# High parts first at a stage's start, half a second unit before the second tile's turn, and two key-value blocks around the first turn

## The reference

```python
# first block: retention and block attention side by side, then a gated FFN
h = rmsnorm(x, norm1_w);  rq, rk, rv, rg, mq, mk, mv, ga, gb = split(h @ w_in)
a = (silu(rg) * retention(rq, rk, rv)) @ w_ret_out
b = moba_attention(mq, mk, mv) @ w_moba_out
x = x + (sigmoid(ga) * a + sigmoid(gb) * b) @ w_o
x = x + (silu(h2 @ w_gate) * (h2 @ w_up)) @ w_down          # h2 = rmsnorm(x, norm2_w)
# second block, two layers i = 0, 1
k_nope, k_rope, v = shared_kv(x, kv_w_down, kv_norm, kv_w_up)  # before layer 1 only
x = post_norm(x, 0.5 * swiglu(x, ffn1_w_in[i], ffn1_w_out[i]), ...)
mix = fox_mixer(x, ...) if i == 0 else mla_mixer(x, w_dq, q_norm, w_uq, w_o, k_nope, k_rope, v, ...)
x = post_norm(x, mix, ...)
x = post_norm(x, 0.5 * swiglu(x, ffn2_w_in[i], ffn2_w_out[i]), ...)
x = post_norm(x, sigmoid(x @ ple_w_gate[i] + b) * (p[i] @ ple_w_proj[i]), ...)
```

## Time and profile before

| | us |
|---|---|
| median of 3 runs | 1618.79 (1617.51 to 1619.44) |
| the profiled execution, its own time | 1619.16 |
| its span in the profile | 1617.4 |
| TensorE busy | 1529.9 |
| VectorE busy | 967.0 |
| ScalarE busy | 793.4 |
| GpSimd busy | 156.4 |

### The profile page before, as it was taken

The page is one execution under the profiler, slowest core; times in us unless marked ns, Lnnn a source line. Parts: engine busy times, 40 slices in busy tenths (PEclk is TensorE's granted clock), DMA queues, the critical chain, the costliest instruction groups (busy, mean ns, idle before and its releaser), DMA issues.

```text
span 1617.4 us, 22095 instructions
## 1 busy us (share of the span) xinstructions
PE 1529.9 (95%) x8416; PEld 1328.2 (82%) x8416; DVE 967.0 (60%) x1305; ACT 793.4 (49%) x961; POOL 156.4 (10%) x46
## 2 busy tenths in 40 slices
PE   6999999999999999899899998999998989999997
PEld 5887788888888887798788886888877877888885
DVE  4566565656556566425566668766665354665667
ACT  4436435444444444554454446544445553544445
POOL 2010011000010001350100001100023332100001
PEclk9999999999999999999999999999998999999999
DMA  7534345655565554432465554565544223565552
GB/s 276 196 134 164 128 159 183 208 192 196 183 191 189 184 197 149 148 131 79 149 203 194 182 202 163 176 218 182 190 161 142 85 102 112 177 208 195 194 192 81
DMA packets 186860, 274.61 MB, mean 170 GB/s; under 512 B 9952, under 2 KB 137056, under 8 KB 186720
## 3 DMA queue, kind: packets, MB, share of 16 engines
q1 hardware_dynamic: 182848, 261.72, 48.1%
q10 hardware_dynamic: 3952, 12.06, 2.4%
HBM read 272.70 MB, written 1.05 MB: 169 GB/s over the span
## 4 chain that ended last, share of the span: by engine, by line
PE 82%; DVE 11%; ACT 4%; issue 1%; POOL 1%; DMA 1%; ACTq 0%; SPq 0%; DVEq 0%
PE bank L588 22%; PE bank L590 11%; PE bank L498 9%; PE bank L500 8%; PE bank L499 8%; PE acc L498 6%; PE acc L499 6%; PE acc L500 6%; DVE w_lo L1474 2%; PE acc L705 2%; ACT w_hi L1035 2%; PE acc L494 2%; DVE x L1525 1%; DVE x L1576 1%; PE bank L494 1%
## 5 line engine op out<-in xcount | busy, mean ns | idle before, releaser
L1474 DVE TENSOR_TENSOR w_lo<-w_raw,w_hi 128x2048 fp32r<-128x2048 f32 x215 | 491.1, 2285 | 217.3 <-ACT w_hi L1111 122.0
L588 PE MATMUL bank<-xT,w_hi 128*128 128x512 f32 x1520 | 379.9, 392 | 0.0
L588 PEld LDWEIGHTS bank<-xT,w_hi 128*128 128x128 f32 x1520 | 276.1, 189 | 51.3
L455 POOL TENSOR_TENSOR w_lo<-w_raw,w_hi 128x2048 fp32r<-128x2048 f32 (+2 forms) x37 | 152.4, 4119 | 1427.6 <-ACT w_hi L1035 1427.6
L1111 ACT ACTIVATE w_hi<-w_raw 128x2048 fp32r<-128x2048 f32 x145 | 276.4, 1907 | 0.0
L498 PE MATMUL bank<-w_hi,xT 128*128 128x512 f32 (+2 forms) x666 | 246.5, 370 | 19.2 <-DVE xT L1515 12.6
L1035 ACT ACTIVATE w_hi<-w_raw 128x2048 fp32r<-128x2048 f32 (+4 forms) x107 | 194.3, 1818 | 98.9 <-PE bank L500 77.1
L500 PE MATMUL bank<-w_hi,xT 128*128 128x512 f32 (+2 forms) x666 | 241.4, 363 | 0.0
L499 PE MATMUL bank<-w_lo,xT 128*128 128x512 f32 (+2 forms) x666 | 241.4, 362 | 0.0
L590 PEld LDWEIGHTS bank<-xT,w_lo 128*128 128x128 f32 x1520 | 207.4, 190 | 14.8
L590 PE MATMUL bank<-xT,w_lo 128*128 128x256 f32 x1520 | 211.9, 282 | 0.0
(11 more groups left out here) (196 smaller groups left out, 1819.2 us busy)
## 6 DMA issues: line engine op xcount, KB each, us to landing
w_raw<-in_ffn_w_in SPq DMA_DIRECT2D x176, 512.0 KB, 4.4
w_raw<-in_ffn_w_out SPq DMA_DIRECT2D x88, 512.0 KB, 4.1
w_raw<-in_w_in SPq DMA_DIRECT2D x52, 512.0 KB, 4.5
w_raw<-in_fox_w_in SPq DMA_DIRECT2D x24, 512.0 KB, 4.6
w_raw<-in_w_ffn_gate SPq DMA_DIRECT2D x22, 512.0 KB, 4.3
w_raw<-in_w_ffn_up SPq DMA_DIRECT2D x22, 512.0 KB, 4.2
w_raw<-in_w_ffn_down SPq DMA_DIRECT2D x22, 512.0 KB, 3.9
w_raw<-in_ple_w_gate SPq DMA_DIRECT2D x16, 512.0 KB, 4.1
```

What stands on the lines that cost most here:

```text
L455: pool.tensor_tensor(w_lo[slot][:, 0:cols], w_raw[slot][:, 0:cols], w_hi[slot][:, 0:cols].bitcast(F32), ALU.subtract).then_inc(w_lo_done[s ...
L588: pe.matmul(out, wh[:, k, m], both, start=k == 0, stop=False)
L1474: nc.vector.tensor_tensor(w_lo[slot][:, 0:cols], w_raw[slot][:, 0:cols], w_hi[slot][:, 0:cols].bitcast(F32), ALU.subtract)\
```

## The change

- `Chunk.run` with `ready` (at sites 0, "mix", 2, 4, 5, 6, 8) and `first` of an FFN: for each unit and tile, all matmuls high x high come first and wait only for `w_hi` and `xTh`; then the matmuls with the weights' low part and those with the activations' low part, in this order for the first unit and in the other for the second. The waits for `w_hi_done` and `w_lo_done` are made for both tiles.
- Half of the second unit's `k` for tile 0 is moved ahead of the second tile's transposes: 6 matmuls in a chunk, 12 in an FFN.
- At site 6 `kv(0)` comes before the transposes of tile 0, `kv(1)` between the two turns instead of after them. ScalarE's copies of the blocks (`keep_kv`), with the splits ahead of them, move likewise. VectorE makes the low part of `dq0`'s first unit before it takes the mean of tile 1.

```diff
@@ class Chunk @@
-                def run(self, *which, tiles=range(T)):
+                def run(self, *which, tiles=range(T), part=None):
...
-                        if which[0] == 0:
+                        if which[0] == 0 and part != 1:
                             take(self.banks[t], ("ev", *self.name, t))
                         for w in which:
                             u, kt = self.us[w], self.kts[w]
                             n = units[u][2]
-                            if t == 0:
-                                pe.wait_ge(w_lo_done[u % RING], u // RING + 1)
...
-                            for j in range(kt):
-                                k = sum(self.kts[:w]) + j
-                                if self.ready is not None:
-                                    need("pe", "xT", self.ready, t, k // 4)
-                                a, tok = self.slot0 + k, slice(t * P, (t + 1) * P)
-                                mm = mm3(bank[self.banks[t]][:, 0:cols.stop - cols.start], self.ah[:, a, tok],
-                                         self.al[:, a, tok], wh[:, j, cols], wl[:, j, cols],
-                                         w == 0 and j == 0, w == last and j == kt - 1)
...
+                            js = (range(kt), range(kt // 2), range(kt // 2, kt))[0 if part is None else part + 1]
+                            k0 = sum(self.kts[:w])
+                            if self.ready is None:
+                                if t == 0:
+                                    pe.wait_ge(w_lo_done[u % RING], u // RING + 1)
+                                for j in js:
+                                    a = self.slot0 + k0 + j
+                                    mm = mm3(out, self.ah[:, a, tok], self.al[:, a, tok], wh[:, j, cols], wl[:, j, cols],
+                                             w == 0 and j == 0, w == last and j == kt - 1)
+                            else:
+                                stop = w == last and js[-1] == kt - 1
+                                pe.wait_ge(w_hi_done, u + 1)
+                                for j in js:
+                                    need("pe", "xTh", self.ready, t, (k0 + j) // 4)
+                                    pe.matmul(out, self.ah[:, self.slot0 + k0 + j, tok], wh[:, j, cols],
+                                              start=w == 0 and j == 0, stop=False)
+
+                                def rest_of_weights(stop):
+                                    pe.wait_ge(w_lo_done[u % RING], u // RING + 1)
+                                    for j in js:
+                                        mm = pe.matmul(out, self.ah[:, self.slot0 + k0 + j, tok], wl[:, j, cols],
+                                                       start=False, stop=stop and j == js[-1])
+                                    return mm
+
+                                def rest_of_x(stop):
+                                    for j in js:
+                                        need("pe", "xT", self.ready, t, (k0 + j) // 4)
+                                        mm = pe.matmul(out, self.al[:, self.slot0 + k0 + j, tok], wh[:, j, cols],
+                                                       start=False, stop=stop and j == js[-1])
+                                    return mm
+
+                                if w:
+                                    rest_of_x(False)
+                                    mm = rest_of_weights(stop)
+                                else:
+                                    rest_of_weights(False)
+                                    mm = rest_of_x(stop)
+                            if part == 0:
+                                continue
@@ tile_steps @@
-                return [lambda: c.run(0, tiles=(0,)), lambda: c.run(1, tiles=(0,)), lambda: c.run(0, 1, tiles=(1,))]
+
+                def early():
+                    c.run(0, tiles=(0,))
+                    c.run(1, tiles=(0,), part=0)
+
+                return [early, lambda: c.run(1, tiles=(0,), part=1), lambda: c.run(0, 1, tiles=(1,))]
@@ ffn of TensorE: first and start @@
-                def first(b, t):
-
+                def first(b, t, ks=range(KD)):
 
                     u = u0 + b
-                    if t == 0:
...
+                    pe.wait_ge(w_hi_done, u + 1)
+                    for k in ks:
+                        need("pe", "xTh", site, t, k // 4)
+                        pe.matmul(out, xTh[:, k, tok], wh[:, k], start=k == 0, stop=False)
...
+                    if b:
+                        rest_of_x(False)
+                        mm = rest_of_weights(True)
+                    else:
+                        rest_of_weights(False)
+                        mm = rest_of_x(True)
                     if t == 1:
                         mm.then_inc(w_used, 1)
...
                     first(0, 0)
+                    first(1, 0, range(KD // 2))
...
                     to_xT(site, src, b0=4, between=start)
-                for b, t in ((1, 0), (0, 1), (1, 1)):
-                    first(b, t)
+                first(1, 0, range(KD // 2, KD))
+                for b in range(2):
+                    first(b, 1)
@@ TensorE, layer 1, site 6 @@
-                    to_xT(6, x, b0=4, between=lambda: kv(0))
+                    kv(0)
+                    to_xT(6, x, b0=4, between=lambda: kv(1))
...
                 else:
-                    kv(1)
                     chunk("dq0", (4, 5), ready=6)
@@ ScalarE @@
-            def norm_and_turn(site, rms=False, first=None, early=None, between=None, b0=0):
+            def norm_and_turn(site, rms=False, first=None, early=None, filler=None, between=None, b0=0):
...
                     split_to(early)
+                if filler is not None:
+                    filler()
                 if site < 9:
                     xT_evac(site, b0=b0, tiles=(0,))
...
-                    norm_and_turn(6, early=split[0] + 1, between=lambda: keep_kv(0), b0=4)
+                    norm_and_turn(6, early=split[0] + 1, filler=lambda: keep_kv(0), between=lambda: keep_kv(1), b0=4)
...
-                    keep_kv(1)
                     ahead("dq0")
@@ VectorE @@
-                norm_and_turn(2 + 4 * l, ffn(1 + 2 * l, ALPHA, ckv_rest if l else None), b0=4)
+                add_half = ffn(1 + 2 * l, ALPHA, ckv_rest if l else None)
+
+                def finish_half(t):
+                    add_half(t)
+                    if l and t:
+                        split_to(unit_at["dq0"][0] + 1)
+
+                norm_and_turn(2 + 4 * l, finish_half, b0=4)
```

More of the change, by code:

```diff
@@ L528, in run @@
                             cols = slice(c0, c0 + min(n, CH))
-                            for j in range(kt):
-                                k = sum(self.kts[:w]) + j
-                                if self.ready is not None:
-                                    need("pe", "xT", self.ready, t, k // 4)
-                                a, tok = self.slot0 + k, slice(t * P, (t + 1) * P)
-                                mm = mm3(bank[self.banks[t]][:, 0:cols.stop - cols.start], self.ah[:, a, tok],
-                                         self.al[:, a, tok], wh[:, j, cols], wl[:, j, cols],
-                                         w == 0 and j == 0, w == last and j == kt - 1)
+                            out = bank[self.banks[t]][:, 0:cols.stop - cols.start]
@@ new lines, in run @@
+                            tok = slice(t * P, (t + 1) * P)
+                            js = (range(kt), range(kt // 2), range(kt // 2, kt))[0 if part is None else part + 1]
[32 more added lines that the diff above has]
+                                    mm = rest_of_x(stop)
@@ L601, in last_up, with rest_of_weights, rest_of_x @@
                     mm.then_inc(w_used, 1)
-                def first(b, t):
+                def first(b, t, ks=range(KD)):
                     u = u0 + b
-                    if t == 0:
-                        pe.wait_ge(w_lo_done[u % RING], u // RING + 1)
-                    wh, wl = (w[u % RING][:, :].rearrange("p (k n) -> p k n", k=KD) for w in (w_hi, w_lo))
-                    for k in range(KD):
-                        need("pe", "xT", site, t, k // 4)
-                        tok = slice(t * P, (t + 1) * P)
-                        mm = mm3(bank[2 * b][:, t * HB:(t + 1) * HB], xTh[:, k, tok], xTl[:, k, tok], wh[:, k], wl[:, k],
-                                 k == 0, k == KD - 1)
+                    wh, wl = (w[u % RING][:, :].rearrange("p (k n) -> p k n", k=KD) for w in (w_hi, w_lo))
+                    tok, out = slice(t * P, (t + 1) * P), bank[2 * b][:, t * HB:(t + 1) * HB]
+                    pe.wait_ge(w_hi_done, u + 1)
+                    for k in ks:
+                        need("pe", "xTh", site, t, k // 4)
+                        pe.matmul(out, xTh[:, k, tok], wh[:, k], start=k == 0, stop=False)
+                    def rest_of_weights(stop):
+                        pe.wait_ge(w_lo_done[u % RING], u // RING + 1)
+                        for k in ks:
```

(9 more changed lines are left out.)

## The result

The changed kernel takes 1604.03 us in the median of 4 runs (1603.91 to 1604.46), against 1619.12 us (1617.51 to 1620.62) for the kernel before: a ratio of 0.991, 95% interval 0.9896 to 0.9923. The profiled execution took 1603.96 us around a span of 1602.2.

What follows compares the result with a forecast made beforehand. TensorE, busy 95% of the span, was taken as the bound, so only waits, clock or issue rate could give time. Terms: 2.3 + 1.5 + 1.4 + 1.0 + 4.0 - 1.7 - 0.1 = 8.4 us, so 1610.4 us; range 1606.0 to 1615.0.

Steps and rivals of the forecast that it cites:

- the key-value blocks: Site 6: dq0 ends 5 us earlier, but VectorE's inverse root meets GpSimd's unit; gain 4.0 us, bounds 2.0 and 8.0.
- The first rival: Key-value blocks: VectorE is not held by GpSimd, gain 8.0 us instead of 4.0, time 1606.4 us; chance 10%.
- up to 0.9 us of wait: dq0, behind the key-value blocks: up to 0.9 us waiting for its second unit's low part, ending at 1232.1.
- The first stage: Site 0: early start gives nothing as the half unit needs GpSimd's unit; 0.1 us lost, plus 1.7 by the clock.
- The order's part of this term: First stage: the second turn stands behind the wait for GpSimd, ending at 30.7 against 30.58; 0.1 us lost.
- The clock's part: First stage: TensorE idles some 2.9 us and its clock is low after it; 1.7 us lost, between 0 and 4.3.
- The FFN starts: At 258, 445 and 1390 us: high products start earlier, gain 0.75 us each, 2.3 in all.
- At 788 us: FFN start, site 3: 36 matmuls instead of 24 fit before the turn, which stays; gain 1.5 us.
- at 635: Forget-gate stage, site 2: six 512-column matmuls move ahead of the turn, GpSimd's unit in time; gain 1.4 us.
- At 1023 us: Site 5: kv_down's gain is lost waiting for GpSimd; eight half-unit products run before GpSimd is done; gain 1.0 us.
- The added waits: Stage starts: semaphore waits taken at 0 while satisfied; a generous bound was 6 us.

Runs made afterwards that it cites:

- clash_back: The kernel after, with only the first half of the fourth kv_up unit loaded, so that its transfer comes early; 1608.66 us.
- kv_only: The kernel before with only the two key-value blocks moved ahead of the turns, and ScalarE's and VectorE's orders that belong to it; 1614.78 us.
- kv_dq_high: The kernel before with two things alone: the move of the key-value blocks, and high part first in dq0, the stage behind them; 1608.16 us.
- no_early_dq: The kernel after without VectorE's early low part of dq0's first unit, which comes behind the low parts of x again; 1612.08 us.
- best: The kernel after without the half unit ahead of the turn at two places, the first stage (rq0) and mla_ob0; 1600.15 us.
- clash_gone: The kernel before, with the low part of the fourth kv_up unit made by VectorE behind its low part of cq, not by GpSimd; 1611.54 us.

## Why the prediction was wrong

**The step that failed** is in the key-value blocks: "GpSimd began 1239.72 - 1237.06 = 2.7 us after dq0's last matmul, which frees the unit's buffer. Now that is 1234.8", and with it "VectorE gets at most an op or two in between". All eleven steps that were left at the end of GpSimd's second unit came in between; GpSimd began its third 1229.70 - 1224.58 = 5.1 us after dq0, not 2.7. I took the end of TensorE's dq0 for what starts that unit. It was not: a load has to land first, issued when VectorE has made the low part of the unit whose raw buffer it takes (1219.57 in the kernel after, as the low part begun at 1217.79 ended). ScalarE wanted it 5.8 us after its issue and had it after 8.1. Before, 9.5 us lay between its issue (1228.19) and its use (1237.74), so it never showed as a wait. It was issued 0.5 us ahead of dq0's first matmul then (1228.71); with the blocks moved ahead it is issued 3.8 us behind it (1215.78), so the load became the last to arrive, though dq0 itself takes no less time than before. Shown from both sides: the load made early brings the stall back (`clash_back`, 4.2 us); dq0 made longer by 1.4 us brings it back without an edit to the load (`kv_only`; its load also took 7.1 us instead of 8.1, but with 8.1 GpSimd would have begun near 1236.1 by my estimate, still ahead of the chain's end at 1236.7); and with the move, dq0's own order of products is enough to remove it (`kv_dq_high`).

The term was mis-sized by this and by the clock: at the transposes of cq, for which it was worked out, the place gave 9.5 us instead of 4.0 (10.1 at VectorE's products, the mark of the table). The first rival had 8.0; the two idle times are 8.24. Some 1.7 us more are the stretch at half speed from 1214 to 1217.5 us, which has no counterpart in the kernel after; 0.45 are lost, as dq0 took 8.80 us instead of 8.35.

The rule of the Trainium skill, "SBUF — State Buffer", "Who interferes with whom", fits every held step in the traces (two SBUF inputs each); what I had wrong was whether the two would meet.

**What I priced by order and missed.** The move is not independent of the order of products. I gave dq0 nothing of its own from high part first, only "up to 0.9 us of wait". Its 1.4 us (8.6 against 10.0 in `kv_only`, first to last matmul) go with whether 4.4 us of stall appear. And I overlooked that `tile_steps` serves mla_ob0 too: 0.5 us lost.

**The first stage.** The order's part of this term, 0.1 us lost, was right to a tenth: GpSimd's unit comes at 22.4 and the stretch ends at 30.74 instead of 30.58. The clock's part, 1.7, did not come; its level in the kernel after, windows of the trace (the third number from the end):

```profile
23.00:31.00 8.00, 8.00 (x41) 6.72 (x40) 4.28 (x4) 4.81 (x4) 0.00 (x0) 1.00 0.79 247
```

After 2.90 us of idling the granted clock was 1.00. But in two of the five profiles with this half unit (`clash_back`, `no_early_dq`) it fell near 22 us, after 2.35 and 2.45 us of idling, and they were 1.6 and 1.5 us later than the kernel after at the first statistics. So the size was right, but I took for certain what happens in some executions, and the length of the idling, by which I chose it, does not tell which: it fell after the shorter ones. Here is `clash_back`:

```profile
20.00:31.00 11.00, 8.65 (x36) 7.21 (x36) 3.67 (x3) 4.11 (x4) 2.41 (x1) 0.84 0.73 232
```

Taken against the kernel without the half unit, the place costs 1.7 us with the clock up, and some 3.2 where it falls: the forecast compared it with the kernel before alone, and called the early start worth nothing.

**The FFN starts** went as described. At 257 us, in the kernel after:

```profile
255.30 4.61 POOL L455 TENSOR_TENSOR w_lo<-w_raw,w_hi 128x2048 fp32r<-128x2048 f32 x1 [30.87 <-ACT w_hi L1090]
...
256.40 1.09 ACT L1099 ACTIVATE xT<-acc 128x512 fp32r<-128x512 f32 x2 [1.18 <-PE acc L494]
...
257.14 1.19 PE L648 MATMUL bank<-w_hi,xT 128*128 128x256 f32 x8 [0.34 <-ACT xT L1099]
```

The first matmul comes 0.74 us after ScalarE's first copy instead of 1.47: 0.7 each at 258 and 445 us (the shift grew from 2.30 ahead of the one to 3.75 behind the other), and 0.8 for the stretch with the start at 1390, 0.75 forecast. At 788 us, 36 matmuls stand before the turn (1.4, forecast 1.5), and at 635 the gain is 1.2 (forecast 1.4), with a wait of 0.17 us for GpSimd that I had at nothing. At 1023 us it is 0.3 of 1.0. The wait for GpSimd is still there, as forecast (1.32 us at 1021.90), and behind it eight products fewer are left, 1.0 us. But the lower clock lasted longer at 1001 to 1011 us, the first turn of x took 1.97 us instead of 1.32, and GpSimd's unit started 6.1 us earlier than before, where the FFN ahead had ended 6.4 earlier, and took 4.89 us instead of 4.57.

**The added waits** cost nothing that shows: the steps of matmuls at the stages' starts are 0.12 and 0.23 us, as before.

**The clock** explains most of the rest. From 95 to 629 us, 4.0 us came where two FFN starts account for 1.4. Windows of the kernel before, then of the kernel after: the same 13 us hold 52 matmuls in the one and 62 in the other.

```profile
178.00:191.00 13.00, 10.87 (x52) 9.30 (x53) 9.07 (x28) 6.09 (x14) 0.00 (x0) 0.74 0.23 81
```

```profile
178.00:191.00 13.00, 10.02 (x62) 8.61 (x63) 9.90 (x28) 6.60 (x17) 0.00 (x0) 1.00 0.24 81
...
124.00:128.00 4.00, 4.00 (x13) 3.13 (x12) 3.56 (x18) 2.40 (x2) 0.00 (x0) 0.60 0.79 260
```

Before, the clock is at its lower level twice in this window, which costs 1.5 and 1.6 us against the kernel after, which in turn loses 0.65 us at 124, where the next wait takes part of it in: 2.5 us net. The reverse happens from 1301 to 1320 us, where the kernel after is at its lower level twice and the kernel before once (1320 to 1323): 2.2 us lost. What sets these places I have not found out. The kernel before showed the same ones twice up to 1220 us, the kernel after throughout; `kv_only` and `kv_dq_high`, with the same program up to 1200 us as the kernel before, each had others, and differed from it by 0.5 and 2.4 us at 629. No change of this size can be read to better than some 2 us from one trace without setting them apart.

## What to carry to other kernels

When a stretch gets shorter, ask of each instruction behind it what released it, and also what would have released it a microsecond later: a load that had 9.5 us and took 8 is the next wait, and it may do good where it keeps a slow engine out of a fast one's chain. The margin here is 0.77 us, and 0.28 in the trace of `best`; giving the unit to VectorE, as in `clash_gone`, would take the clash away rather than dodge it. Work ahead of a turn pays only where its operands are there before the turn could start: at 635 and 788 us some 1.4 each, at the first stage and mla_ob0 a loss.

## What was unexpected of the hardware

- A stall can cost more than its length. After 3.56 us of idling TensorE ran at a granted 0.50 until 1255 us; in the second trace of the same kernel the stretch from 1246 to 1255 us had 0.81. In all seven traces with a held step the clock fell behind it, for 3.4 to 10.3 us; in the seven without one it fell there in three, for 3.4 us. With the stall gone (`clash_gone`) 4.3 us of stall were worth 6.3 us by the traces; the medians' 7.5 hold 0.7 us from before the place.
- A 2-element step with two SBUF inputs, started behind GpSimd's unit, was held for 4.4 to 4.5 us in seven traces. VectorE's products for cq read PSUM and one SBUF tile: in `best` the second of them started 0.3 us behind GpSimd's unit and took 0.61 us, no longer than elsewhere. The Trainium skill, "SBUF — State Buffer", "Who interferes with whom", has this distinction, by the number of SBUF inputs, for instructions outside the two-port modes; the traces of these steps agree. But the chain's first step, a `tensor_scalar` with one SBUF input, was held too: 1.24 to 1.31 us beside GpSimd's second unit in all fourteen traces, where one of the same kind on 8 elements takes 0.17 us without GpSimd (at 125 us). Whether it ran in such a mode, no run here shows.
- At the start the clock fell in two executions and not in three, and the two had the shorter idling (2.35 and 2.45 us against 2.90, 2.90 and 3.12). Where it falls costs some 1.5 us there. What decides is open.
